# Rotary turn of queries and keys in the mixer: from products with a rotation matrix to small DMAs between partitions

## The chip, the cores and the metric

The kernel runs on one core of one Trainium2 chip. The metric is device time in microseconds (us) of one launch. Three timed runs of the kernel before gave 1842.23, 1841.44 and 1841.96, median 1841.96. In the text PE is TensorE, DVE is VectorE, ACT is ScalarE, POOL is GpSimd and SP is SyncE.

## The reference, cut to what matters

The program is a block of two transformer stacks on 512 tokens of width 1024, in float32: feed-forward, a mixer of dilated attention and pooling, feed-forward, then a retention layer and a stick-breaking attention layer. The change touches only the rotary embedding of the mixer's attention, 12 heads of 64 rows of which the first 16 turn:

```python
def apply_partial_rope(x, cos, sin):
    xf = x.astype(jnp.float32)
    half = ROT_DIM // 2                      # ROT_DIM = 16
    x1, x2 = xf[..., :half], xf[..., half:ROT_DIM]
    c, s = cos[None, :, None, :], sin[None, :, None, :]
    out = jnp.concatenate([x1 * c - x2 * s, x2 * c + x1 * s, xf[..., ROT_DIM:]], axis=-1)
    return out.astype(x.dtype)
...
    q = apply_partial_rope(q, cos, sin)
    k = apply_partial_rope(k, cos, sin)
```

The attention that follows uses q and k in scores, an exponential and a product with the values; its result is mixed over three groups of heads.

## The kernel before, in words

Features lie on the 128 partitions and the 512 tokens along the free dimension. A float32 product is made of three PE passes (`passes`, L2580 to L2582): each operand is split by ACT into a rounded high part and by DVE into the rest (`x_hi`, `x_lo`, `w_hi`, `w_lo`). Weights come in slabs of 128x2048: SP fetches a slab into a ring of two (`raw`), ACT writes `w_hi` (`prep`, L740), DVE writes `w_lo` (L1457), and PE uses it for two tiles of eight chunks of three passes.

The mixer does its attention in two halves, each with `qk(last)`, values, and `attend`. A half has six tiles of projected rows, named here (g, o): group g = 0, 1, 2 and o = 0 for queries, 1 for keys. A tile holds two heads, in partitions 0 to 63 and 64 to 127. In the half `qk(False)` the tiles (0,0) and (0,1) are projected together; in `qk(True)` the tile (0,0) was projected ahead, in a bank of `att`.

For each tile, in program order on each engine:

- PE projects the tile into a bank of PSUM (`acc`, four banks).
- ACT copies it, rounded, to `stage_hi` (`rope_split`, L761). DVE writes the rest to `stage_lo` (`rope_low`, L1481) and the tile times the cosines to `tmp` (`rope_cos`, L1796).
- PE, behind the projection of the next tile, multiplies both parts with the constant matrix `rot_r`, which exchanges rows 0 to 7 of a head with rows 8 to 15 and turns a sign (`rotate`, L2752 and L2753).
- DVE multiplies this product by the sines (L1805) and adds (L1808); ACT writes the rounded result (L972, L977, L980: `k_hi`, `q_pair`, `q_both` or `k_both`), and DVE the rest (L1811, L1814, L1819: `k_lo`, `q_pair`, `q_low` or `k_rest`). This is `rope_done`.

So `rope_done` of one tile stands behind `rope_split` and `rope_cos` of the next tile on ACT and DVE. An exception is the end of `qk(True)`: there `rope_done` of (2,0) comes ahead of the split of (2,1), and PE turns (2,0) in the middle of projecting (2,1), and (2,1) in the middle of the values. After the key tiles ((0,1) and (1,1)) ACT and DVE also prepare the next weight slab (`prep`).

POOL's queue then moves queries between partition halves (`q_head<-q_pair` and others), and PE's first scores of a half wait for these DMAs and for the last `k_lo`. Behind `rope_done` of (2,1) DVE prepares weights, forms operands, and takes the maxima of the first scores (`neg_max`, L1853), on which ACT's exponentials (L1013) and then PE wait. Every engine works its own list in order; the waits between engines are semaphores.

`rope_turned` and `rope_in`, which the change adds, lie over the same memory as `stage`. `stage` is used again by `attend` for the turned probabilities.

Of the kernel before, what the change touches and what calls it, by code (L numbers as in the profile page):

```python
# [24 lines left out]
P = 128  # L25
# [30 lines left out]
DIL = 4  # L56
UNITS = 2 * DIL
# [60 lines left out]
def block_kernel(nc, dram, out):  # L118
    with ExitStack() as ctx:
# [34 lines left out]
        rot_r = sb("rot_r", [P, P], F32R)  # L154
# [6 lines left out]
        signs = tmp[:, 4 * TOK:4 * TOK + 3 * P].rearrange("p (k c) -> p k c", k=3)  # L161
# [88 lines left out]
        with ExitStack() as scope:  # L250
# [13 lines left out]
            with ExitStack() as inner:  # L264
# [3 lines left out]
                va = sb("va", [P, TB, N_GROUPS * GROUP_HEADS, 2, HEAD], F32R, inner)  # L268
                stage = sb("stage", [P, 4 * KEYS], F32R, inner)
# [96 lines left out]
        stage_hi, stage_lo = stage[:, 0:2 * KEYS], stage[:, 2 * KEYS:]  # L366
# [73 lines left out]
        rest_clear = sem("rest_clear")  # L440
        h_back = sem("h_back")
# [196 lines left out]
        def _(pool):  # L638
# [26 lines left out]

            pool.wait_ge(park_landed, 16)
# [61 lines left out]
        def _(act):  # L728
# [230 lines left out]
            def rope_split(o, side=False):  # L959

                src = att[:, b.k % BANKS, :] if side else acc[:, u.k % BANKS, :]
                split_acc(stage_hi[:, o * TOK:(o + 1) * TOK], src, 1)
                s.next()
                (b if side else u).next()

            def rope_done(g, o):
                b.next()
# [15 lines left out]
            def qk(last):  # L983
                for g in range(N_GROUPS):
                    for o in range(2):
# [461 lines left out]
        def _(dve):  # L1447
# [332 lines left out]
            nc.vector.tensor_copy(rot_r[:], signs[:, 0, :])  # L1780
            nc.vector.tensor_copy(tri_r[:], signs[:, 1, :]).then_inc(att_free, BANKS)
            nc.vector.tensor_copy(ones_r[:], signs[:, 2, :]).then_inc(const_ready, 1)
# [11 lines left out]
            def rope_cos(o, side=False):  # L1794
                src = att[:, b.k % BANKS, :] if side else acc[:, u.k % BANKS, :]
# [4 lines left out]
            both, lows = Count(), Count()  # L1800
# [23 lines left out]
            def qk(last):  # L1824
                for g in range(N_GROUPS):
                    for o in range(2):
                        if (g, o) == (0, 0):
                            prep()
                            if not last:
                                rstd_of()  # L1830
                                dve.wait_ge(mix_landed, 6 * 16)
                                rope_low(0)

# [5 lines left out]
                        if last or (g, o) != (0, 0):  # L1839
                            rope_low(o, last and (g, o) == (0, 0))  # L1840
# [714 lines left out]
        def _(pe):  # L2555
# [192 lines left out]
            def rotate(o):  # L2748

                dst = side_bank()  # L2750
                cols = slice(o * TOK, (o + 1) * TOK)
                mm(dst, rot_r[:], stage_hi[:, cols], start=True, stop=False)  # L2752
                mm(dst, rot_r[:], stage_lo[:, cols], start=False, stop=True).then_inc(att_full, 1)  # L2753

            def qk(last, ahead=None):
                for g in range(N_GROUPS):
# [8 lines left out]
                    for o in range(2):  # L2765
                        if last and (g, o) == (N_GROUPS - 1, 1):
                            dst = bank()
                            for c in range(DC):
                                if c == DC // 2:
                                    pe.wait_ge(op_ready, op.at())  # L2770
                                    rotate(0)
                                    op.next(2)
# [97 lines left out]
            for i in range(4):  # L2870
# [3 lines left out]
                if i == 0:  # L2874
                    rotate_last()
# [535 lines left out]
```

## Time and profile before

| | us |
|---|---|
| median of three timed runs | 1841.96 |
| the profiled execution, its own time | 1841.76 |
| span of its trace | 1839.9 |
| PE busy in the span | 1823.6 (99%) |
| DVE busy | 1395.1 (76%) |
| ACT busy | 929.8 (51%) |
| POOL busy | 81.5 (4%) |

The profile is one execution. Start times count from the start of the span. Busy times leave out the issuing of DMAs. The mixer's two attention halves lie at about 358 to 460 us and 460 to 535 us. A row of the timeline gives start, duration, engine, line, operation, output <- input, shape and count; in brackets stands how long the engine was idle before it, and what released it.

### The profile page before, as it was taken

Reading aid. Unit: us, or ns where it says so; the run is one execution under the profiler, and the core shown is the slowest. Engines: PE = TensorE matmul, PEld = TensorE weight load, DVE = VectorE, ACT = ScalarE, POOL = GpSimd, SP = SyncE. Lnnn points to the kernel's source line nnn. Section 1 sums busy time; section 2 is a strip of 40 time slices with the busy share of each in tenths; the row PEclk is TensorE's granted clock in tenths of the full one; section 3 lists DMA queues with packets and bytes.
Section 4 is the critical chain, followed back from the end, with each engine's and each line's share of the span. In section 5 each row is a group of like instructions: output and inputs, shape, how many; then the busy total and the mean of one; then the engine's idle time right before and its main releaser. Section 6 shows DMA issues by size and latency. Waiting matters only on the chain.

```text
span 1839.9 us, 28202 instructions
## 1 busy us (share of the span) xinstructions
PE 1823.6 (99%) x11335; PEld 1632.7 (89%) x11341; DVE 1395.1 (76%) x1912; ACT 929.8 (51%) x1274; POOL 81.5 (4%) x109
## 2 busy tenths in 40 slices
PE   9999999999999999999999999999999999999997
PEld 7998998888889988988998899988888888888886
DVE  8875887888778878866888987776767776666566
ACT  6652664435355536643663555455547644444445
POOL 0000000020001000000000000000000000000000
PEclk9999999999999999999999999999999999999999
DMA  6744763462407535743753688732232222221223
GB/s 215 180 125 131 200 165 112 175 152 73 118 24 208 156 106 148 197 148 106 196 140 108 186 217 252 235 125 93 91 138 71 69 92 72 89 88 71 91 69 92
DMA packets 60594, 244.78 MB, mean 133 GB/s; under 512 B 6864, under 2 KB 9456, under 8 KB 49856
## 3 DMA queue, kind: packets, MB, share of 16 engines
q1 hardware_dynamic: 46016, 199.25, 32.3%
q0 software_dynamic: 14032, 43.38, 12.4%
q8 instruction: 80, 1.31, 0.3%
q10 hardware_dynamic: 432, 0.56, 0.1%
q14 instruction: 34, 0.28, 0.0%
HBM read 223.76 MB, written 13.11 MB: 129 GB/s over the span
## 4 chain that ended last, share of the span: by engine, by line
PE 93%; DVE 3%; ACT 1%; issue 1%; DMA 0%; DVEq 0%; ACTq 0%; POOL 0%
PE acc L2580 17%; PE acc L2582 17%; PE acc L2581 17%; PE acc L2588 9%; PE acc L2586 9%; PE acc L2587 9%; PE att L2581 2%; PE att L2582 2%; PE att L2580 2%; PE att L2588 1%; PE att L2586 1%; PE att L2587 1%; PE acc L2855 1%; PE acc L2830 1%; DVE w_lo L1457 0%
## 5 line engine op out<-in xcount | busy, mean ns | idle before, releaser
L1457 DVE TENSOR_TENSOR w_lo<-raw,w_hi 128x2048 fp32r<-128x2048 f32 (+1 forms) x106 | 238.9, 2254 | 56.8 <-ACT w_hi L740 56.5
L740 ACT ACTIVATE w_hi<-raw 128x2048 fp32r<-128x2048 f32 (+1 forms) x106 | 199.3, 1880 | 74.8 <-PE acc L2582 61.0
L2580 PE MATMUL acc<-x_hi,w_hi 128*128 128x512 f32 x488 | 193.1, 396 | 1.5 <-DVE x_lo L1520 1.2
L2582 PE MATMUL acc<-x_hi,w_lo 128*128 128x512 f32 x488 | 190.2, 390 | 0.0
L2581 PE MATMUL acc<-x_lo,w_hi 128*128 128x512 f32 x488 | 190.1, 390 | 0.0
L2586 PE MATMUL acc<-xt_hi,w_hi 128*128 128x256 f32 x684 | 189.1, 276 | 0.0
L2588 PE MATMUL acc<-xt_hi,w_lo 128*128 128x256 f32 x684 | 189.1, 276 | 0.0
L2587 PE MATMUL acc<-xt_lo,w_hi 128*128 128x256 f32 x684 | 189.0, 276 | 0.0
L839 ACT ACTIVATE tmp<-acc 128x256 f32<-128x256 f32 x228 | 86.9, 381 | 120.1 <-PE acc L2588 114.9
L2581 PE MATMUL acc<-g_lo,w_hi 128*128 128x512 f32 x352 | 137.0, 389 | 0.0
L2580 PE MATMUL acc<-g_hi,w_hi 128*128 128x512 f32 x352 | 137.0, 389 | 0.0
L2582 PE MATMUL acc<-g_hi,w_lo 128*128 128x512 f32 x352 | 136.9, 389 | 0.0
L2588 PEld LDWEIGHTS acc<-xt_hi,w_lo 128*128 128x128 f32 x684 | 128.4, 188 | 0.0
L2587 PEld LDWEIGHTS acc<-xt_lo,w_hi 128*128 128x128 f32 x684 | 128.4, 188 | 0.0
L2586 PEld LDWEIGHTS acc<-xt_hi,w_hi 128*128 128x128 f32 x684 | 128.3, 188 | 0.0
L2580 PEld LDWEIGHTS acc<-x_hi,w_hi 128*128 128x128 f32 x488 | 91.6, 188 | 23.1 <-issue 3.4
L2588 PE MATMUL acc<-x_hi,wc_lo 128*128 128x256 f32 x400 | 110.6, 276 | 0.0
L2586 PE MATMUL acc<-x_hi,wc_hi 128*128 128x256 f32 x400 | 110.6, 276 | 0.0
L2587 PE MATMUL acc<-x_lo,wc_hi 128*128 128x256 f32 x400 | 110.5, 276 | 0.0
L2581 PEld LDWEIGHTS acc<-x_lo,w_hi 128*128 128x128 f32 x488 | 91.6, 188 | 20.2 <-issue 1.4
L2582 PEld LDWEIGHTS acc<-x_hi,w_lo 128*128 128x128 f32 x488 | 91.6, 188 | 19.3
L796 ACT ACTIVATE wc_hi<-raw_c 128x1024 fp32r<-128x1024 f32 x57 | 60.4, 1059 | 50.9 <-PE acc L2588 50.9
(512 smaller groups left out, 5123.6 us busy)
## 6 DMA issues: line engine op xcount, KB each, us to landing
raw<-in_ffn_down SPq DMA_DIRECT2D x32, 704.0 KB, 4.1
raw_c<-in_ffn_seven SPq DMA_DIRECT2D x37, 512.0 KB, 5.3
raw<-in_ffn_seven SPq DMA_DIRECT2D x33, 512.0 KB, 4.4
raw<-in_ffn_seven POOLq DMA_DIRECT2D x33, 512.0 KB, 7.4
raw<-in_ffn_seven SPq DMA_DIRECT2D x37, 256.0 KB, 4.4
raw<-in_ret_values SPq DMA_DIRECT2D x8, 1024.0 KB, 4.8
raw<-in_ret_out SPq DMA_DIRECT2D x8, 1024.0 KB, 6.6
raw<-in_sb_v SPq DMA_DIRECT2D x8, 1024.0 KB, 4.8
```

The source lines that it names most:

```text
L740: nc.scalar.activation(w_hi[:, slot, at:at + cols], raw[:, slot, 0:cols], ACT.Copy).then_inc(w_hi_ready, 1)
L796: nc.scalar.activation(wc_hi[:, cols], raw_c[:, third, :], ACT.Copy).then_inc(wc_hi_ready, 1)
L839: nc.scalar.activation(dst, src, ACT.Copy).then_inc(snap_ready, 1)
L1457: tt(w_lo[:, slot, at:at + cols], raw[:, slot, 0:cols], w_hi[:, slot, at:at + cols].bitcast(F32), ALU.subtract).then_inc(w_ready, 1)
L2580: mm(dst, still[0], move[0], start=first, stop=False)
L2581: mm(dst, still[0], move[1], start=False, stop=False)
L2582: return mm(dst, still[1], move[0], start=False, stop=last)
L2586: mm(dst, still[0], move[0], start=first, stop=False, skip_group_check=True)
L2587: mm(dst, still[0], move[1], start=False, stop=False, skip_group_check=True)
L2588: return mm(dst, still[1], move[0], start=False, stop=last, skip_group_check=True)
L2830: last = nc.tensor.transpose(dst[i // TB][:, P * (i % TB):P * (i % TB) + P], tmp[:, at:at + P], ident[:])
L2855: last = mm(dst, va[:, k_blk, value_slot(g, head)].rearrange("p s d -> p (s d)"), turned_probs[:, k % 2, i].rearrange("p s q -> p (s q)"), ...
```

## The change

The rotated rows are no longer made by a product. ACT copies the tile unrounded to `rope_in`, waits for its own copy, and issues four DMAs of 8 partitions x 512 elements (16 KB) each on its own queue. They write the exchanged rows into `rope_turned`, whose other rows are zero. The sign has moved into the table of sines. DVE multiplies `rope_turned` by the sines, after a wait for the four DMAs of the tile. The 12 pairs of products, the 12 DVE subtractions for `stage_lo`, and the matrix `rot_r` with its cast are gone. POOL clears `rope_turned` (128x1024) once per half: behind the first feed-forward, and behind the last product of the first `attend`.

```diff
 # POOL
+            pool.wait_ge(seg_done, FFN_SEGS[0])
+            nc.gpsimd.memset(rope_turned[:], 0.0).then_inc(turned_clear, 1)
+            pool.wait_ge(turned_clear, 1)
             pool.wait_ge(park_landed, 16)
...
+            pool.wait_ge(mixed, UNITS)
+            nc.gpsimd.memset(rope_turned[:], 0.0).then_inc(turned_clear, 1)
             other_halves(1)
 # ACT
             def rope_split(o, side=False):
                 src = att[:, b.k % BANKS, :] if side else acc[:, u.k % BANKS, :]
-                split_acc(stage_hi[:, o * TOK:(o + 1) * TOK], src, 1)
+                act.wait_ge(seg_done, s.at(1))
+                nc.scalar.activation(rope_in[:, o, :], src, ACT.Copy).then_inc(rope_copied, 1)
...
+            def rope_turn(o, half):
+                act.wait_ge(rope_copied, copied.next())
+                act.wait_ge(turned_clear, half + 1)
+                for first in range(0, P, HEAD):
+                    for j in range(2):
+                        to, src = (slice(first + ROT * i, first + ROT * (i + 1)) for i in (j, 1 - j))
+                        act.dma_start(rope_turned[to, o, :], rope_in[src, o, :]).then_inc(turned_landed[o], 16)
...
                         rope_split(o, last and (g, o) == (0, 0))
+                        rope_turn(o, int(last))
                         if o == 1 and g < N_GROUPS - 1:
                             prep()
 # DVE
-            def rope_low(o, side=False):
-                cols = slice(o * TOK, (o + 1) * TOK)
-                src = att[:, b.k % BANKS, :] if side else acc[:, u.k % BANKS, :]
-                settle()
-                low(stage_lo[:, cols], src, stage_hi[:, cols])
             def rope_cos(o, side=False):
                 src = att[:, b.k % BANKS, :] if side else acc[:, u.k % BANKS, :]
+                settle()
+                dve.wait_ge(rope_copied, copied.next())
                 tt(t(o), src, rope_a[:, 0, :], ALU.mult).then_inc(att_free if side else acc_free, 1)
...
             def rope_done(g, o, split_after):
-                dve.wait_ge(att_full, b.next())
-                tt(t(2 + o), att[:, (b.k - 1) % BANKS, :], rope_a[:, 1, :], ALU.mult).then_inc(att_free, 1)
-                dve.wait_ge(att_free, b.at(BANKS))
+                dve.wait_ge(turned_landed[o], 4 * 16 * shifted[o].next())
+                link(tt(t(2 + o), rope_turned[:, o, :], rope_a[:, 1, :], ALU.mult))
 # PE
-            def rotate(o):
-                dst = side_bank()
-                cols = slice(o * TOK, (o + 1) * TOK)
-                mm(dst, rot_r[:], stage_hi[:, cols], start=True, stop=False)
-                mm(dst, rot_r[:], stage_lo[:, cols], start=False, stop=True).then_inc(att_full, 1)
...
-                        if (g, o) != (0, 0):
-                            pe.wait_ge(op_ready, op.at(0 if g else 1))
-                            rotate(1 - o)
```

On ACT, from the square root at the head of `qk(False)` (L768 before, L779 after) to the first weight slab behind the tile (1,1), the kernel before has:

```order
L768 ACTIVATE tmp<-att,eps 128x512
L761 ACTIVATE stage<-acc 128x512 x2
L740 ACTIVATE w_hi<-raw 128x2048
L980 ACTIVATE q_both<-tmp 64x512 x2
L761 ACTIVATE stage<-acc 128x512
L980 ACTIVATE k_both<-tmp 64x512 x2
L761 ACTIVATE stage<-acc 128x512
L740 ACTIVATE w_hi<-raw 128x2048
```

The same place on ACT in the changed kernel:

```order
L779 ACTIVATE tmp<-att,eps 128x512
L974 ACTIVATE rope_in<-acc 128x512
L987 DMA rope_turned<-rope_in 8x512 x4
L974 ACTIVATE rope_in<-acc 128x512
L987 DMA rope_turned<-rope_in 8x512 x4
L751 ACTIVATE w_hi<-raw 128x2048
L1002 ACTIVATE q_both<-tmp 64x512 x2
L974 ACTIVATE rope_in<-acc 128x512
L987 DMA rope_turned<-rope_in 8x512 x4
L1002 ACTIVATE k_both<-tmp 64x512 x2
L974 ACTIVATE rope_in<-acc 128x512
L987 DMA rope_turned<-rope_in 8x512 x4
```

Eight DMA issues now stand ahead of the first `w_hi`, and eight more ahead of the second, which follows the last row shown.

On DVE, at the end of `qk(True)` from the query tile (2,0) on, the kernel before has:

```order
L1805 TENSOR_TENSOR tmp<-att,rope_a 128x512
L1808 TENSOR_TENSOR tmp<-tmp 128x512
L1814 SCALAR_TENSOR_TENSOR q_pair<-tmp,q_pair 128x256 x2
L1481 TENSOR_TENSOR stage<-acc,stage 128x512
L1796 TENSOR_TENSOR tmp<-acc,rope_a 128x512
L1805 TENSOR_TENSOR tmp<-att,rope_a 128x512
L1808 TENSOR_TENSOR tmp<-tmp 128x512
L1811 SCALAR_TENSOR_TENSOR k_lo<-tmp,k_hi 128x512
L1457 TENSOR_TENSOR w_lo<-raw,w_hi 128x1536
```

And in the changed kernel:

```order
L1824 TENSOR_TENSOR tmp<-rope_turned,rope_a 128x512
L1826 TENSOR_TENSOR tmp<-tmp 128x512
L1832 SCALAR_TENSOR_TENSOR q_pair<-tmp,q_pair 128x256 x2
L1814 TENSOR_TENSOR tmp<-acc,rope_a 128x512
L1824 TENSOR_TENSOR tmp<-rope_turned,rope_a 128x512
L1826 TENSOR_TENSOR tmp<-tmp 128x512
L1829 SCALAR_TENSOR_TENSOR k_lo<-tmp,k_hi 128x512
L1480 TENSOR_TENSOR w_lo<-raw,w_hi 128x1536
```

One subtraction is gone, and the second product with the sines (the key tile (2,1)) reads `rope_turned`, whose rows come by DMAs issued only after ACT's copy of that tile.

## Rows read from the trace of the kernel before

**Rows 1.** The page, part 1 and part 4 (chain that ended last).

```profile
PE 1823.6 (99%) x11335; PEld 1632.7 (89%) x11341; DVE 1395.1 (76%) x1912; ACT 929.8 (51%) x1274; POOL 81.5 (4%) x109
PE 93%; DVE 3%; ACT 1%; issue 1%; DMA 0%; DVEq 0%; ACTq 0%; POOL 0%
```

**Rows 2.** Timeline of PE round the second rotation of `qk(False)`.

```profile
364.62 0.40 PE L2752 MATMUL att<-stage,rot_r 128*128 128x512 f32 x1
365.10 0.40 PE L2580 MATMUL acc<-x_hi,w_hi 128*128 128x512 f32 x1
```

**Rows 3.** The two longest entries of PE's waits, 345 to 535 us: total, times, longest.

```profile
PE att L2752 <- DVE stage L1481: 0.9, 2, 0.5
PE att L2814 <- DMA q_head<-q_pair: 0.8, 1, 0.8
```

**Rows 4.** Timeline of ACT and SP's queue: DMA issues on the hardware queues.

```profile
0.76 0.40 ACTq L925 DMA_DIRECT2D gains<-in_gains  x1
1.19 1.00 ACTq L927 DMA_DIRECT2D h<-in_x  x2
...
811.36 0.33 SPq L491 DMA_DIRECT2D tmp<-in_ffn_seven  x1
...
813.16 0.62 SPq L472 DMA_DIRECT2D raw<-in_ffn_down  x1
```

**Rows 5.** Issue to landing, of the lines L925 (36 KB) and L927 (256 KB).

```profile
DMA to landing us min/median/max: 1.7/1.7/1.7
DMA to landing us min/median/max: 4.1/4.7/5.2
```

**Rows 6.** Timeline of POOL, first half.

```profile
357.68 1.81 POOL L670 MEMSET q_head<- 64x2048 f32 x1
```

**Rows 7.** Timeline of ACT, first half.

```profile
358.31 1.91 ACT L740 ACTIVATE w_hi<-raw 128x2048 fp32r<-128x2048 f32 x1
...
370.74 1.27 ACT L980 ACTIVATE k_both<-tmp 64x512 fp32r<-64x512 f32 x2 [3.49 <-DVE tmp L1808]
...
425.72 0.84 ACT L1006 ACTIVATE va<-acc,r_tok 128x256 fp32r<-128x256 f32 x2 [0.24 <-PE acc L2582]
```

**Rows 8.** Timeline of DVE, first half.

```profile
361.71 2.28 DVE L1457 TENSOR_TENSOR w_lo<-raw,w_hi 128x2048 fp32r<-128x2048 f32 x1
...
373.48 0.69 DVE L1481 TENSOR_TENSOR stage<-acc,stage 128x512 fp32r<-128x512 f32 x1
...
374.69 2.28 DVE L1457 TENSOR_TENSOR w_lo<-raw,w_hi 128x2048 fp32r<-128x2048 f32 x1
...
389.01 2.29 DVE L1457 TENSOR_TENSOR w_lo<-raw,w_hi 128x2048 fp32r<-128x2048 f32 x1 [1.11 <-ACT w_hi L740]
...
424.17 0.68 DVE L1457 TENSOR_TENSOR w_lo<-raw,w_hi 128x512 fp32r<-128x512 f32 x1
```

**Rows 9.** Timeline of ACT, second half.

```profile
468.08 0.60 ACT L761 ACTIVATE stage<-acc 128x512 fp32r<-128x512 f32 x1 [3.85 <-PE acc L2582]
468.57 1.91 ACT L740 ACTIVATE w_hi<-raw 128x2048 fp32r<-128x2048 f32 x1
```

**Rows 10.** Timeline of DVE, second half.

```profile
483.50 2.28 DVE L1457 TENSOR_TENSOR w_lo<-raw,w_hi 128x2048 fp32r<-128x2048 f32 x1
...
496.94 0.69 DVE L1805 TENSOR_TENSOR tmp<-att,rope_a 128x512 f32<-128x512 f32 x1 [0.23 <-PE att L2753]
...
499.06 0.69 DVE L1811 SCALAR_TENSOR_TENSOR k_lo<-tmp,k_hi 128x512 fp32r<-128x512 f32 x1 [0.70 <-ACT k_hi L972]
```

**Rows 11.** Timeline of PE: first and third scores of the second half.

```profile
500.41 0.27 PE L2814 MATMUL att<-classes,ident_b 128*128 128x256 bf16 x1 [0.78 <-DMA q_head<-q_pair]
...
508.85 0.27 PE L2814 MATMUL att<-classes,ident_b 128*128 128x256 bf16 x1
```

**Rows 12.** Busy time by window: PE, PEld, DVE, ACT, POOL, then granted clock, DMA share, GB/s.

```profile
1831.00:1833.00 2.00, 0.00 (x0) 0.00 (x0) 1.44 (x4) 1.02 (x3) 0.59 (x1) 1.00 0.95 184
1835.00:1837.00 2.00, 0.00 (x0) 0.00 (x0) 0.00 (x0) 0.00 (x0) 0.00 (x0) 0.50 0.87 266
```

More of the change, by code:

```diff
@@ L56 @@
 DIL = 4
+ROT = HEAD // 8
 UNITS = 2 * DIL
@@ L153, in block_kernel @@
         mean_d = sb("mean_d", [P, P])
-        rot_r = sb("rot_r", [P, P], F32R)
         tri_r = sb("tri_r", [P, P], F32R)
@@ L268, in block_kernel @@
                 va = sb("va", [P, TB, N_GROUPS * GROUP_HEADS, 2, HEAD], F32R, inner)
+                with ExitStack() as under:
+                    rope_in = sb("rope_in", [P, 2, TOK], F32, under)
+                    rope_turned = sb("rope_turned", [P, 2, TOK], F32, under)
                 stage = sb("stage", [P, 4 * KEYS], F32R, inner)
@@ L440, in block_kernel @@
         rest_clear = sem("rest_clear")
+        rope_copied = sem("rope_copied")
+        turned_clear = sem("turned_clear")
+        turned_landed = [sem(f"turned_landed{o}") for o in range(2)]
         h_back = sem("h_back")
@@ L1779, in _ @@
             dve.wait_ge(const_landed, 4 * 16)
-            nc.vector.tensor_copy(rot_r[:], signs[:, 0, :])
-            nc.vector.tensor_copy(tri_r[:], signs[:, 1, :]).then_inc(att_free, BANKS)
-            nc.vector.tensor_copy(ones_r[:], signs[:, 2, :]).then_inc(const_ready, 1)
+            nc.vector.tensor_copy(tri_r[:], signs[:, 0, :]).then_inc(att_free, BANKS)
+            nc.vector.tensor_copy(ones_r[:], signs[:, 1, :]).then_inc(const_ready, 1)
             dve.wait_ge(const_ready, 1)
@@ L1838, in qk @@
                             rope_done(g, 0, 0)
-                        if last or (g, o) != (0, 0):
-                            rope_low(o, last and (g, o) == (0, 0))
                         rope_cos(o, last and (g, o) == (0, 0))
@@ L2765, in qk @@
                     for o in range(2):
[L2766 to L2772, printed above, removed]
-                                done = passes(dst, w(DC + c), (x_hi[:, c, :], x_lo[:, c, :]), c == 0, c == DC - 1)
-                            done.then_inc(seg_done, 1)
-                            continue
                         if g or last and o:
                             project(w, o * DC, x)
-                        if (g, o) != (0, 0):
-                            pe.wait_ge(op_ready, op.at(0 if g else 1))
-                            rotate(1 - o)
-                            op.next(2)
                         elif last:
                             gather(units_done, 1)
-            def rotate_last(behind=0):
-                pe.wait_ge(op_ready, op.at(behind))
-                rotate(1)
-                op.next(2)
+                op.next(2 * N_GROUPS)
             def gather(done, filled):
@@ L2908, in _ @@
             qk(True, ahead[0])
-            values(x, plain, {(0, DC - 1): lambda: rotate_last(1), (1, DC - 1): lambda: first_score(1),
+            values(x, plain, {(1, DC - 1): lambda: first_score(1),
                               (2, DC - 1): lambda: scores(1, 1)})
@@ L3357, in constants @@
     c["diag_neg"] = np.where(i >= j, f(NEG), f(0))
-    half = HEAD // 8
-    rot = np.zeros((P, P), f)
-    for m in range(P):
-        d = m % HEAD
-        if d < half:
-            rot[m + half, m] = -1
-        elif d < 2 * half:
-            rot[m - half, m] = 1
+    half = ROT
     c["fold"] = np.hstack([np.zeros((P, HEAD), f), np.vstack([np.eye(HEAD, dtype=f)] * 2), np.zeros((P, HEAD), f)])
-    c["signs"] = np.stack([rot, (i >= j).astype(f), np.ones((P, P), f)], 1)
+    c["signs"] = np.stack([(i >= j).astype(f), np.ones((P, P), f)], 1)
     pos = np.arange(TOK, dtype=f)
@@ L3373, in constants @@
             ang = pos * inv[m % HEAD % half]
-            cos[m], sin[m] = np.cos(ang), np.sin(ang)
+            cos[m], sin[m] = np.cos(ang), np.sin(ang) * f(1 if m % HEAD >= half else -1)
     c["rope_a"] = np.stack([cos, sin], 1).reshape(P, 2, P, DIL).transpose(0, 1, 3, 2).reshape(P, 2, TOK)
```

13 lines of the change are left out of this document (5 added, 8 removed).

## The prediction

> **What bounds the kernel now.** I read the page first: PE is busy for 99% of the span and carries 93% of the chain that ended last [rows 1]. So whatever leaves PE's list could be worth its full time, and whatever is added to DVE or ACT seems free. That is an average, so I then read PE's waits in the stage of the change: from 345 to 535 us the only waits of more than 0.2 us are 0.9 for the operands of the rotation and 0.8 for the queries' DMA [rows 3]. The reader should see two things: PE has almost no slack to lose, and each wait is short because DVE and ACT are just in time. The third view is the timelines of ACT and DVE. In the first half DVE works from 361.71 to 424.85 with hardly a gap that PE causes [rows 8]: its short gaps are round trips to ACT, as before the slab at 389.01. At 425.72 ACT is only 0.24 us ahead of PE [rows 7]. In the second half a run of ACT and DVE work goes from ACT's copy at 468.08, which PE released, to the last `k_lo` at 499.75 [rows 9, 10], and PE starts the first scores 0.7 us later [rows 11]. So the chain through ACT and DVE decides in both halves, and PE arrives together with it.
>
> **What goes.** Twelve rotations leave PE. One takes 365.10 - 364.62 = 0.48 us of its list [rows 2]; a matmul's own 0.40 overlaps with the next. That is 12 x 0.48 = 5.8 us, and 0.9 of waiting before two of them [rows 3]: 6.7 us for PE alone. DVE loses 12 subtractions of 0.69 [rows 8], start to start 0.6, about 0.7 of its list with the signal that each costs. The cast of `rot_r` is at 22 us and under other work: nothing.
>
> **What comes.** Each tile puts four DMA issues on ACT behind its copy. The trace has issues on ACT of 0.40 and 0.50 us, and four on SP in a row that take 813.16 - 811.36 = 1.80 us [rows 4]. All of these have 128 partitions; the new ones have 8. The durations hardly follow the size, so I take 1.8 us for four, plus 0.1 for ACT's wait for its own copy (my estimate: the hand-overs between engines in these rows are below 0.1). Ends: 0.33 each (SP's shortest), 1.35 for four; and 0.52 each (ACT's, rounded up), 2.1. If the cost is by partitions, 8 instead of 128, it would be near 0.1 each. An issue to landing took 1.7 us for 36 KB and 4.7 for 256 KB [rows 5]; for 16 KB I take 1.7, with 4.7 as the far end. The clearings of POOL stand behind work that ended, and the second must be over when ACT wants to issue at 461: POOL clears 64x2048 in 1.81 us [rows 6], so 1024 columns should take about 1 and surely below 2, from PE's last product of the half at 459; and ACT is idle for 3.85 us before 468.08 [rows 9], which covers the delay of its copies. Nothing for them.
>
> **First half.** All times are on the clock of the trace before. ACT: copy of (0,0) to 357.7, wait and issues to 359.6, copy of (0,1) to 360.2, issues to 362.1, `w_hi` 1.9 to 364.0. It was done at 360.2 [rows 7]. DVE starts `w_lo` at 364.05 instead of 361.71 [rows 8]: +2.3. On to the tile (1,1) one subtraction is gone: +1.6. There ACT, after `k_both`, now needs 0.6 copy + 0.1 + 1.8 + 1.9 = 4.4 us until `w_hi` is there. `k_both` ends at 372.0 before [rows 7] and 373.6 now, so `w_lo` starts at 378.05 instead of 374.69: +3.35. Two more subtractions go: the slab of 389.01 starts at 390.95, +1.95. Then the pooling is the same DVE and ACT chain as before, and its weights end at 426.8 instead of 424.85. The 0.24 us that ACT waited for PE [rows 7] absorb a part: **+1.7 us**. PE, 3.6 us ahead by then (six rotations and the missing wait), loses this lead in waits for weight slabs and goes on with the chain.
>
> **Second half.** ACT's copy at 468.08 is released by PE, so it starts level. Issues to 470.5, `w_hi` to 472.4 instead of 470.48: `w_lo` +2.0. Less one subtraction: +1.25. At (1,1) again 4.4 us after `k_both`: `w_lo` at 486.45 instead of 483.50 [rows 10], +2.95. Less one: the `k_lo` of (1,1) and the `q_pair` of (2,0) +2.1. ACT then copies (2,1) from 496.65 to 497.2 and issues until 499.1; the last DMA starts at 498.65 and lands 1.7 later, 500.35. DVE multiplies by the sines at 500.4 instead of 496.94 [rows 10], and the last `k_lo` ends at 503.2 instead of 499.75: **+3.45 us**. Queued behind that one DVE wait are the branch weights, three sums, the values and the two maxima, in all the chain that releases the third scores, at 508.85 before [rows 11]: also +3.45. PE meanwhile reaches the first scores at 496.2 (2.9 from six rotations and 0.5 of waiting less), waits 7 us, then has 8.2 us of work, done at 511.4; the third scores are released at 512.3. Its lead is gone here too.
>
> Sum: 1841.76 + 1.7 + 3.45 = 1846.9. The 7 us wait may cost more: with PE idle at the end of the trace, the granted clock is 1.00 and then 0.50 [rows 12], that is 2.4 and then 1.2 GHz. PE has 0.9 us in hand behind the wait; half speed over a third of its 8.2 us of work costs 2.7, which leaves 1.8 if the clock falls. I give that one chance in three, +0.6. Forecast: **1847.5**, 5.7 above the profiled execution and 5.5 above the median of the runs (the execution lies 0.2 below it).
>
> The Trainium skill (DMA: Bandwidth & Descriptors, section Issuing engines are not separate DMA queues) says that the time a sequencer needs to start a DMA is usually small relative to the DMA itself. Here it isn't: four issues take 1.80 against 1.7 to landing [rows 4, 5]. By the rule the issues would count little, as in the second rival.
>
> **Rivals.**
> 1. *All is hidden.* PE is at 99% and decides alone: 1841.76 - 6.7 = 1835.1. For it speaks the page [rows 1], and that `rope_done` comes a whole tile of projection after the copy. Against it: the tile (2,1) has no tile behind it, and 389.01 to 424.85 is DVE's own chain. 5%.
> 2. *Issues are cheap* (0.1 each, 0.4 for four), the case on the fast side of the chain. Then `w_hi` is never late, and DVE gains 0.4 at the first slab and 0.6 to 0.7 per tile: 2.1 at the end of the first half. In the second the missing subtractions are nearly used up by the landing of (2,1): DMAs from 494.1 land at 496.3, `k_lo` ends 0.5 earlier. 1841.76 - 2.6 = 1839.2. It decides where four issues take less than about 1.0 us. For it: 8 rows instead of 128. Against: 36 KB and 256 KB differ by a tenth of a microsecond on ACT [rows 4]. 20%.
> 3. *The clock falls.* PE's 8.2 us behind the wait take twice as long: it reaches the third scores at 503.25 + 16.3 = 519.5 instead of 512.3: 1846.9 + 7.2 = 1854.1. It needs the idle stretch to be long enough and the return slow; no row shows the return. 8%. The Trainium skill (TensorE: Matmul & The Clock Gate, its table of rules at the end) warns that a long idle gap between bursts of matmuls brings the clock down to half; by it the fall is certain here, and the forecast would be 1848.7 with the return as I took it.
> 4. *Landing is slow* (4.7 us beside the weight loads): the last sines wait 3.0 longer, in the first half the tile (2,0) about 2: 1846.9 + 5 = 1852. 12%.
>
> The forecast holds with 55%. Its own range comes from the ends of the issue cost. Three blocks of four issues stand in the deciding chain of each half, six in all: 5.15 - 6 x 0.45 = 2.5 at 1.35 us, 5.15 + 6 x 0.3 = 6.95 at 2.1 us, and up to 1.8 for the clock, so 1844.2 to 1850.5. The whole range to hold 8 in 10 takes in a part of the slow landing and of cheap issues: 1840.5 to 1853.5. A measurement of this kernel tells about 0.2%, 3.7 us, from no change. Faster by more (below 1838.3): rival 1 and a little of 2, 8%. Within: most of rival 2 and the low side of the forecast, 27%. Slower: 65%.
>
> **What would show it.** Timeline of ACT: four issues of 0.4 to 0.5 us behind each copy; at 0.1 rival 2 is right. DVE's slabs (before at 374.69 and 483.50) start 3 us late against ACT's copies. PE's waits in the stage grow from below 2 to some 13 us, the longest about 7 before the first scores of the second half, released by `k_lo`, with `turned_landed` behind it. If PE's waits stay below 3 us, the chain did not bind, and I am wrong. A granted clock below 1.00 in 500 to 515 us speaks for rival 3. Outside 345 to 535 us nothing should change.

## The result, and the profile after

| | before | after |
|---|---|---|
| median of 5 runs each, us | 1841.76 | 1862.49 |
| range of them, us | 1841.19 to 1842.23 | 1859.60 to 1863.01 |
| profiled execution, us | 1841.8 | 1859.6 |
| its span, us | 1839.9 | 1857.8 |

The ratio is 1.0105, 95% interval 1.0094 to 1.0117: the change makes the kernel 20.7 us slower. The direction was forecast, the size (5.7 us) was not, and the measured time lies outside the range given. The two profiled executions differ by 17.9 us in their spans, and that is the difference which the rows below can account for.

The page after, part 1 and part 4, against [rows 1]:

```profile
PE 1820.6 (98%) x11317; PEld 1629.8 (88%) x11317; DVE 1388.8 (75%) x1899; ACT 929.7 (50%) x1274; POOL 83.3 (4%) x111
PE 90%; DVE 4%; ACT 2%; issue 1%; ACTq 1%; DMA 1%; DVEq 0%
```

PE and DVE work less, as the change intends, and only POOL works more, 83.3 against 81.5 us. DVE, ACT, the issues and the DMAs have taken some 3% of the deciding chain from PE. PE's waits, 345 to 560 us (total, times, longest), against [rows 3]:

```profile
PE att L2802 <- DVE k_lo L1829: 13.9, 1, 13.9
PE acc L2594 <- DVE w_lo L1480: 9.3, 4, 3.7
```

The waits grew from 1.9 to 23.4 us. They have the two places that the prediction named, with 13.9 us in place of 7 before the first scores. (Each sum takes in 0.2 us for `o_even`, which is the same in both.) Next ACT's timeline, first half and (from 490.21) second half. Its rows of before are [rows 7, 9]; ACTq rows are its DMA issues, and 2.61 is the time of four of them.

```profile
357.79 3.23 ACTq L987 DMA_DIRECT2D rope_turned<-rope_in  x4
361.07 0.60 ACT L974 ACTIVATE rope_in<-acc 128x512 f32<-128x512 f32 x1 [3.31 <-issue]
361.70 2.61 ACTq L987 DMA_DIRECT2D rope_turned<-rope_in  x4
364.41 1.92 ACT L751 ACTIVATE w_hi<-raw 128x2048 fp32r<-128x2048 f32 x1 [2.74 <-PE acc L2596]
...
490.21 2.62 ACTq L987 DMA_DIRECT2D rope_turned<-rope_in  x4
492.93 1.92 ACT L751 ACTIVATE w_hi<-raw 128x2048 fp32r<-128x2048 f32 x1 [2.75 <-issue]
...
499.68 3.95 ACTq L987 DMA_DIRECT2D rope_turned<-rope_in  x4
503.68 0.63 ACT L994 ACTIVATE k_hi<-tmp 128x512 fp32r<-128x512 f32 x1 [4.03 <-issue]
...
508.47 2.67 ACTq L987 DMA_DIRECT2D rope_turned<-rope_in  x4
```

A block of four issues takes 2.6 to 3.95 us, not 1.8, and ACT does nothing beside it here. The block of tile (2,0), at 499.68, also holds `k_hi` of the tile before, which the prediction had not counted. DVE's timeline shows where this arrives, against [rows 8, 10]:

```profile
366.36 2.29 DVE L1480 TENSOR_TENSOR w_lo<-raw,w_hi 128x2048 fp32r<-128x2048 f32 x1 [3.90 <-ACT w_hi L751]
...
381.39 2.29 DVE L1480 TENSOR_TENSOR w_lo<-raw,w_hi 128x2048 fp32r<-128x2048 f32 x1 [3.15 <-ACT w_hi L751]
...
390.03 0.69 DVE L1829 SCALAR_TENSOR_TENSOR k_lo<-tmp,k_hi 128x512 fp32r<-128x512 f32 x1 [1.51 <-ACT k_hi L994]
...
391.84 0.69 DVE L1824 TENSOR_TENSOR tmp<-rope_turned,rope_a 128x512 f32<-128x512 f32 x1 [0.39 <-DMA rope_turned<-rope_in]
...
395.83 2.29 DVE L1480 TENSOR_TENSOR w_lo<-raw,w_hi 128x2048 fp32r<-128x2048 f32 x1 [1.12 <-ACT w_hi L751]
...
494.88 2.29 DVE L1480 TENSOR_TENSOR w_lo<-raw,w_hi 128x2048 fp32r<-128x2048 f32 x1 [3.16 <-ACT w_hi L751]
...
504.34 0.69 DVE L1829 SCALAR_TENSOR_TENSOR k_lo<-tmp,k_hi 128x512 fp32r<-128x512 f32 x1 [2.33 <-ACT k_hi L994]
...
505.88 0.69 DVE L1824 TENSOR_TENSOR tmp<-rope_turned,rope_a 128x512 f32<-128x512 f32 x1 [0.85 <-DMA rope_turned<-rope_in]
...
514.01 0.69 DVE L1824 TENSOR_TENSOR tmp<-rope_turned,rope_a 128x512 f32<-128x512 f32 x1 [4.54 <-DMA rope_turned<-rope_in]
...
516.12 0.69 DVE L1829 SCALAR_TENSOR_TENSOR k_lo<-tmp,k_hi 128x512 fp32r<-128x512 f32 x1 [0.70 <-ACT k_hi L994]
```

The slab of 389.01 [rows 8] starts at 395.83: +6.82 at the end of the first half's chain, of which 6.46 is still there when ACT makes the first copy that PE releases in the second (474.54 against 468.08 in [rows 9]). The last `k_lo` starts at 516.12 against 499.06 [rows 10]: +17.06.

The granted clock, by window (columns as in [rows 12]), and PE's first and third scores, whose first row of before is in [rows 11] by the other product of the pair:

```profile
384.00:386.00 2.00, 2.00 (x5) 1.56 (x6) 1.27 (x3) 0.95 (x2) 0.00 (x0) 0.50 0.63 152
...
502.00:504.00 2.00, 0.95 (x9) 0.75 (x7) 0.00 (x1) 0.33 (x1) 0.00 (x0) 1.00 1.01 208
504.00:506.00 2.00, 0.00 (x0) 0.00 (x0) 0.81 (x2) 0.30 (x1) 0.00 (x0) 1.00 0.18 32
506.00:508.00 2.00, 0.00 (x0) 0.00 (x0) 1.27 (x3) 0.67 (x2) 0.00 (x0) 0.63 0.00 0
...
510.00:512.00 2.00, 0.00 (x0) 0.00 (x0) 0.00 (x0) 0.00 (x0) 0.22 (x1) 0.50 0.89 182
...
516.00:520.00 4.00, 3.12 (x12) 2.66 (x13) 3.19 (x3) 2.19 (x4) 0.00 (x0) 0.50 0.00 0
520.00:522.00 2.00, 2.00 (x18) 2.00 (x17) 1.97 (x3) 0.00 (x0) 0.00 (x0) 0.95 0.82 250
```

```profile
516.88 0.61 PE L2802 MATMUL att<-band,ident_b 128*128 128x512 bf16 x1 [13.92 <-DVE k_lo L1829]
...
527.02 0.39 PE L2802 MATMUL att<-band,ident_b 128*128 128x512 bf16 x1
```

PE stops at 503, the clock goes to 0.50 (1.2 GHz) at 508 and is back near 1.00 at 520, 3 us after work resumed. First to third scores take 10.14 us, before 508.85 - 500.41 = 8.44 [rows 11]. The clock also fell in the first half, to 0.50 over 384 to 386, behind a wait of 3.7 us for `w_lo`; before, it was at 1.00 all through the stage. What that first fall cost, no run separates.

### The profile page after: what moved, and what is told of

It is laid out like the page before. It is cut to its first block, busy times and chain, and to the rows that moved or that the text cites. A ratio compares the mean times of both kernels' runs of the same rounds, so it can differ in the third digit from the quotient of the medians.

```text
span 1857.8 us, 28198 instructions
## 1 busy us (share of the span) xinstructions
PE 1820.6 (98%) x11317; PEld 1629.8 (88%) x11317; DVE 1388.8 (75%) x1899; ACT 929.7 (50%) x1274; POOL 83.3 (4%) x111
## 4 chain that ended last, share of the span: by engine, by line
PE 90%; DVE 4%; ACT 2%; issue 1%; ACTq 1%; DMA 1%; DVEq 0%
PE acc L2594 17%; PE acc L2595 16%; PE acc L2596 16%; PE acc L2601 9%; PE acc L2600 9%; PE acc L2602 9%; PE att L2595 2%; PE att L2596 2%; PE att L2594 2%; PE att L2601 1%; PE att L2602 1%; PE att L2600 1%; ACTq L987 1%; PE acc L2844 1%; PE acc L2819 1%
```

## The experiments

All are edits of the changed kernel unless said otherwise. The theory: the issues on ACT are the main cost, through what stands behind them; second the landing of a tile's rows where nothing covers it; third the clock. In the expectations, A is always the theory as it stood then.

**e1_no_dmas.** The four-issue loop of `rope_turn` is taken out, and with it DVE's wait; the exchanged rows stay zero.

```diff
-                for first in range(0, P, HEAD):
-                    for j in range(2):
-                        to, src = (slice(first + ROT * i, first + ROT * (i + 1)) for i in (j, 1 - j))
-                        act.dma_start(rope_turned[to, o, :], rope_in[src, o, :]).then_inc(turned_landed[o], 16)
...
-                dve.wait_ge(turned_landed[o], 4 * 16 * shifted[o].next())
```

> The changed kernel without its 48 small DMAs and without DVE's wait for them; the copies, the clearing by POOL and all else stay. Left out: the exchanged rows are zero, so the rotary turn is not computed. Theory A (the DMA issues hold ACT's queue and make the weight slabs and the last key tile late; the chain through ACT and DVE decides): the time falls to about 1839, 2.7 below the kernel before, since DVE's chain gains only its missing subtractions. Rival B (PE's list decides alone, the issues only disturb it): 1835.1, all 6.7 us of the removed products. If neither the issues nor the landing is the cause, the time stays near 1862.

Measured: 1840.61 (1839.80 to 1842.11), ratio 0.9992 [0.9982, 1.0001]. All the loss hangs on the DMAs. But even free of their cost the change gains almost nothing, though 6.7 us are gone from PE. I first read that as A, yet 2.8 us of what is missing was the clock, as e12_none_busy shows below.

**e2_two_dmas.** `for first in (0,):`, so two of four issues; the other head's rows are missing.

> The changed kernel with two of the four DMAs of a tile (the rows of the second head are not exchanged), the wait counted for two. A block of issues on ACT takes 1.3 us instead of 2.6. Theory A (issues on ACT's queue): seven to eight decisive blocks, each 1.3 shorter, less of the lost clock: about 1850. Rival C (the landing of the DMAs decides, 2 to 3.5 us from the last issue): one issue pair less matters only where DVE waits for a landing, twice, so 1859 to 1861.

Measured: 1850.90 (1848.86 to 1851.06), ratio 1.0046 [1.0029, 1.0063]. Half of the issues give back 11.6 of the 20.7 us: the cost goes with the number of issues.

**e3_16_rows.** Four issues of 16 partitions by half the columns, from and to the same partitions, in place of 8 by all (the rows are not exchanged).

> The changed kernel with four DMAs a tile as before and 16 KB each, but each moves 16 partitions x 256 elements on the same partitions instead of 8 x 512 to others (the rows are copied unexchanged). The question is why an issue takes 0.63 us instead of the 0.40 to 0.50 of the 128-partition DMAs. If a DMA over fewer than 16 partitions costs the queue more, the issue falls to 0.40 to 0.47, a block to 1.8, and the time to what I forecast for that cost, 1847 to 1850. If source and destination in SBUF or the queue of ACT in this stage make it slow, the issue stays at 0.63 and the time at 1862.

Measured: 1859.16 (1858.04 to 1861.52), ratio 1.0088 [1.0072, 1.0105]; 0.612 us for an issue (median) against 0.632. Twice the partitions change little. The interval overlaps that of the changed kernel.

**e4_sp_queue.** The four issues are made by SP between its loads of weights:

```diff
-                        act.dma_start(rope_turned[to, o, :], rope_in[src, o, :]).then_inc(turned_landed[o], 16)
+                        sp.dma_start(rope_turned[to, o, :], rope_in[src, o, :]).then_inc(turned_landed[o], 16)
```

> The changed kernel with the same 48 DMAs issued on SP's queue, in an order that keeps them between the weight loads as they fall due. Theory A: ACT's copies and weight slabs are on time again, so the first half gains about 2 on the kernel before; in the second the last key tile still waits for four issues (2.6) and a landing (2 to 3) behind its copy, about 3 later than before: 1840 to 1846. Rival C (landing and traffic of the small DMAs beside the weight loads): the moves are as late as before the edit, over 1855.

Measured: 1845.27 (1844.40 to 1846.01), ratio 1.0017 [1.0007, 1.0027]. An issue takes SP 0.625 us too, but nothing waits behind it: 17.2 us come back. DVE's timeline of this kernel, to compare with [rows 8, 10]:

```profile
386.81 2.29 DVE L1484 TENSOR_TENSOR w_lo<-raw,w_hi 128x2048 fp32r<-128x2048 f32 x1 [1.11 <-ACT w_hi L766]
...
490.78 0.69 DVE L1828 TENSOR_TENSOR tmp<-rope_turned,rope_a 128x512 f32<-128x512 f32 x1 [2.02 <-DMA rope_turned<-rope_in]
...
498.87 0.69 DVE L1828 TENSOR_TENSOR tmp<-rope_turned,rope_a 128x512 f32<-128x512 f32 x1 [4.50 <-DMA rope_turned<-rope_in]
...
500.99 0.69 DVE L1833 SCALAR_TENSOR_TENSOR k_lo<-tmp,k_hi 128x512 fp32r<-128x512 f32 x1 [0.69 <-ACT k_hi L999]
```

The first half's chain is now 2.2 us earlier than before (386.81 against 389.01). In the second the lead has grown to 3.85 us at the `k_lo` of (1,1) (488.06 against 491.91). Two waits for rows lose it again, 2.02 us at the tile (2,0) and 4.50 at the last tile, and the last `k_lo` is 1.93 us late.

**e8_weights_first.** Only the order on ACT: the split of the next weights ahead of the issues.

```diff
-                        rope_turn(o, int(last))
                         if o == 1 and g < N_GROUPS - 1:
                             prep()
+                        rope_turn(o, int(last))
```

> The changed kernel, with ACT's split of the next projection's weights (w_hi, 1.91 us) ahead of the key tile's four issues in place of behind them, so that DVE's w_lo no longer waits 3.90 us for it; the rows leave 1.9 us later. Theory A (the issues cost by what stands behind them on ACT): at the key tiles w_hi is 2.6 us earlier and the landing 1.9 us later, where DVE has work to cover it: some 2.5 us a tile come back at three of the tiles (1,1) and (2,1) and (0,1) of each half, less the last tile's later landing: 1850 to 1857. Rival B (the landing is what decides, the issue's place does not matter): 1862 to 1866, as slow as the change or slower.

Measured: 1851.39 (1849.82 to 1852.31), ratio 1.0047 [1.0031, 1.0062]. Moving one line gives back 11 us. ACT's timeline shows a reason that I had not expected:

```profile
361.89 1.91 ACT L751 ACTIVATE w_hi<-raw 128x2048 fp32r<-128x2048 f32 x1
362.03 2.61 ACTq L987 DMA_DIRECT2D rope_turned<-rope_in  x4
```

The issues run while the activation ahead of them works. I had expected the rows to leave 1.9 us later; they leave 0.14 us behind the start of `w_hi`. So a block costs ACT its full length only where an instruction behind it is due.

**e7_shapes.** The groups of four take six shapes in turn; `few` is 8 partitions, `table` the rotation table in DRAM. DVE gets other rows than the exchanged ones.

```diff
+                kind = turns[0] % 6
+                    if kind == 0:
+                        act.dma_start(room[few, o, :], rope_in[few, o, :]).then_inc(turned_landed[o], 16)
+                    elif kind == 1:
+                        act.dma_start(room[few, o, :], table[few, o, :]).then_inc(turned_landed[o], 16)
...
```

> The twelve tiles' groups of four issues on ACT take six shapes in turn: 8 partitions by 2 KB from SBUF, the same from DRAM, 16 partitions by 2 KB from SBUF, the same from DRAM, 128 partitions by 128 bytes from SBUF, the same from DRAM. The rows that DVE takes are then not the exchanged ones, so the values are others; the waits are the same. Theory A (an issue costs ACT more for a source in SBUF than for one in DRAM): some 0.61 to 0.63 us each from SBUF, 0.33 to 0.50 us from DRAM, whatever the rows. Rival B (it costs by the partitions, the 128-partition ones being the cheap ones): 0.63 us for 8 partitions of either source, under 0.5 us for 128 partitions of either source. Rival C (it costs by what stands ahead on the queue, the first of a group less than the later ones): the same in all six, with the later of a group dearer.

Measured: 1855.37 in a single run; what counts are its rows. The answers for the six lines, in ns min/median/max: 8 partitions, then 16, then 128, each from SBUF (`rope_in`) and from DRAM (`in_rope_a`):

```profile
L993 ACTq DMA_DIRECT2D rope_turned<-rope_in x8: 632/642/1264, 357.4 to 467.7; - x8
L995 ACTq DMA_DIRECT2D rope_turned<-in_rope_a x8: 287/312/324, 361.3 to 474.2; - x8
L997 ACTq DMA_DIRECT2D rope_turned<-rope_in x8: 555/612/1022, 370.3 to 484.4; - x8
L999 ACTq DMA_DIRECT2D rope_turned<-in_rope_a x8: 332/436/442, 375.1 to 488.3; - x8
L1001 ACTq DMA_DIRECT2D rope_turned<-rope_in x8: 522/626/1357, 383.7 to 498.1; - x8
L1003 ACTq DMA_DIRECT2D rope_turned<-in_rope_a x8: 352/452/453, 388.1 to 505.4; - x8
```

Theory A: 0.61 to 0.64 us from SBUF at any number of partitions, 0.31 to 0.45 from DRAM. No issue from DRAM (at most 0.453 us) reaches the shortest one from SBUF (0.522). In this run the query tiles have the source in SBUF and the key tiles that in DRAM, so by itself it can't tell source from tile. The changed kernel can: there both kinds of tile copy from SBUF, and both take 2.61 to 2.62 us for four where nothing lengthens them. So of what was varied it is the source in SBUF that makes an issue dear. Why the chip takes longer for it is not shown here.

**e10_small_heads.** GpSimd's last two copies of `q_head` carry 8 partitions instead of 64, so that they leave the DMA engines to the last tile's rows.

```diff
+                        rows = slice(own[j].start, own[j].start + 8) if a and g else own[j]
-                        pool.dma_start(q_head[j][own[j], :, g, :], q_pair[own[j], :, :]).then_inc(head_landed, 16)
+                        pool.dma_start(q_head[j][rows, :, g, :], q_pair[rows, :, :]).then_inc(head_landed, 16)
```

> The changed kernel, where in the second half GpSimd's last two copies of the query heads (q_head, 256 KB each, issued at 509.05 while the last tile's exchanged rows are under way) carry 8 partitions each in place of 64; the scores of those heads are computed from zeros for the rest. Theory A (the last tile's rows land 2.87 us behind the end of their issues because they share the DMA engines with those copies, share 0.81 to 0.97 over 510 to 513): the landing falls to 1.7 us or less, DVE's wait from 4.54 to about 3.4 us. Rival B (a row exchange takes 2.9 us by itself): the wait stays at 4.3 to 4.6 us.

One run of 1859.89 us, so the rows of its trace decide. The last block of issues and the DVE instruction that waits for it:

```profile
509.63 2.61 ACTq L988 DMA_DIRECT2D rope_turned<-rope_in  x4
```

```profile
513.64 0.69 DVE L1825 TENSOR_TENSOR tmp<-rope_turned,rope_a 128x512 f32<-128x512 f32 x1 [3.01 <-DMA rope_turned<-rope_in]
```

From the end of the issues to DVE it takes 513.64 - 512.24 = 1.40 us, in the changed kernel 514.01 - 511.14 = 2.87. The sharing costs 1.5 us there. The Trainium skill (DMA: Bandwidth & Descriptors, section Issuing engines are not separate DMA queues) says that DMAs of all engines run on the same 16 DMA engines and interleave. The trace agrees: GpSimd's copies and ACT's rows stood in each other's way, with a DMA share of 0.89 over 510 to 512, against 0.24 with the small copies.

**e11_two_queues.** e4_sp_queue with two of the last tile's four issues on ACT.

> e4_sp_queue (48 issues on SP's queue), with two of the four issues of the last tile (2,1) of each half on ACT, where nothing stands behind them but a step that waits for that tile itself. Theory A (an issue costs its 0.62 us one after another on a queue, and the last tile's issues are on the path): the block on each queue is 1.25 us in place of 2.5, DVE's wait of 4.50 us for the last tile falls by about 1.2 to 3.3 us, and the time is 1843.5 to 1844.5 against 1845.3. Rival B (the landing, not the issue, sets the last tile, so that rows issued earlier land no earlier): wait still 4.3 to 4.6 us, 1845 to 1846.

Measured: 1845.18 (1843.42 to 1846.99), ratio 1.0018 [1.0009, 1.0028]. Neither: DVE's wait fell from 4.50 to 3.86 us, half of what A said, and the time is the same as in e4_sp_queue. Part of what the issues save is taken by a later landing: from the end of the last issue to DVE it takes 498.40 - 495.02 = 3.38 us, in e4_sp_queue 498.87 - 496.05 = 2.82.

**e5_hybrid.** e4_sp_queue, but tiles (2,0) and (2,1) of the second half are rotated by PE, as before:

```diff
-                            rope_done(g, 0)
-                        rope_split(o, last and (g, o) == (0, 0))
+                            rope_done(g, 0, True)
+                        rope_split(o, last and (g, o) == (0, 0), last and g == N_GROUPS - 1)
...
+            def rotate(behind):
+                pe.wait_ge(op_ready, op.at(behind))
+                dst = side_bank()
+                mm(dst, rot_r[:], stage_hi, start=True, stop=False)
+                mm(dst, rot_r[:], stage_lo, start=False, stop=True).then_inc(att_full, 1)
```

> The 48 issues stand on SP's queue, as in e4_sp_queue, and in the second half alone tiles (2,0) and (2,1) are rotated by PE with a product as in the kernel before: their copy is again split for PE, their eight DMAs are gone and two of the twelve 0.48 us products are back. Theory A (what e4_sp_queue had left over was the landing of the last tile of the second half, 4.50 us of DVE idle before sines at 498.87, while its first half had gained 2.2 us and its second had lost it again): the second half's last tile takes as long as before, the first half's 2.2 us stay, PE's wait for k_lo falls from 8.9 to about 3 us, and the time is about 2 to 4 us under the kernel before, 1838 to 1840. Rival B (the 2.2 us of the first half are taken back in any case, by a later wait that does not hang on the rotation, such as a load or the end of DVE's row): no difference from before, 1841 to 1843.

Measured: 1839.19 (median of 11 runs, 1838.37 to 1842.00) against 1842.33 (15 runs, 1841.58 to 1843.16): ratio 0.9984 [0.9975, 0.9993]. It is faster than the kernel before, by 3.1 us. It leaves out nothing, but it is no longer the change as made: only ten of the twelve tiles go through DMAs, from SP's queue. PE's waits in the stage, and the last `k_lo`, 3.00 us earlier than in [rows 10]:

```profile
PE att L2786 <- DVE stage L1516: 2.1, 2, 1.6
PE acc L2615 <- DVE w_lo L1492: 1.9, 1, 1.9
PE att L2836 <- DMA q_head<-q_pair: 1.2, 1, 1.2
```

```profile
496.06 0.69 DVE L1850 SCALAR_TENSOR_TENSOR k_lo<-tmp,k_hi 128x512 fp32r<-128x512 f32 x1 [0.70 <-ACT k_hi L1007]
```

**e6_busy_wait and e9_busy_longer.** What the clock adds: products that nobody reads are put where PE waits, 48 in the one and 62 in the other.

```diff
+                if a:
+                    pe.wait_ge(att_free, b.at(2))
+                    for _ in range(48):
+                        mm(att[:, b.k % BANKS, :], ident_b[:], by_rows(band[:, 0:TB, :]), start=True, stop=True)
```

> The changed kernel, with 48 bf16 products of 512 columns put ahead of the second half's first scores, into a bank that the scores clear again, so that PE works (some 10 us) where it waited 13.9 us for k_lo. It leaves out nothing. Theory A (the wait costs by the late k_lo; the fallen clock adds only the 1.1 us by which the third scores moved more than k_lo did, 18.17 against 17.06): 1860.5 to 1862.5, 1 us less or nothing. Rival B (the halved clock is what makes the size of the loss, as the third rival had it, since PE also does its work behind the wait at half speed): 7 us less, 1855 to 1857.

Measured: 1862.27 (1861.14 to 1864.18), ratio 1.0111 [1.0095, 1.0126]. It says nothing on the clock: PE still waited 3.7 us behind them, and the clock fell all the same, as the next expectation says.

> As e6_busy_wait, with 62 products in place of 48: there they ended at 513.32 (10.53 us, 0.219 us each), PE waited 3.75 us more, and the granted clock still fell (0.59 over 516 to 520, 0.55 over 520 to 524), so that run did not hold the clock. Now they end near 516.4, PE waits about 0.6 us. It leaves out nothing. Theory A (the fallen clock adds only the 1.1 us by which the third scores moved more than k_lo): the granted clock stays at 1.00 over 504 to 524, and the time is 1860.5 to 1862. Rival B (the clock makes up several us of the loss, by what PE does at half speed behind the wait): 1855 to 1858.

Measured: 1860.23 (1858.06 to 1860.99), ratio 1.0097 [1.0080, 1.0114]. The clock was 1.00 in every window from 500 to 524. The first and third scores:

```profile
519.38 0.39 PE L2802 MATMUL att<-band,ident_b 128*128 128x512 bf16 x1 [0.77 <-DVE k_lo L1829]
...
528.03 0.39 PE L2802 MATMUL att<-band,ident_b 128*128 128x512 bf16 x1
```

From the one to the other it took 528.03 - 519.38 = 8.65 us in place of 10.14: in the profiled execution the clock adds 1.5 us to the loss, and rival B (5 us or more) falls. The price is not the same everywhere: in e10_small_heads, e3_16_rows and e6_busy_wait, whose clock fell too, the stretch took 10.82, 11.02 and 11.48 us. The interval of the times overlaps that of the changed kernel, so this rests on the rows. (The 18.17 us in these expectations sets one product of a pair against the other; 508.85 less the 0.23 between the two in a pair gives 18.40, so 1.3 us more than `k_lo`.)

**e12_none_busy and e13_sp_busy.** The same with 18 products in e1_no_dmas and 38 in e4_sp_queue. In e1_no_dmas PE had waited 4.3 us, and the granted clock was:

```profile
495.00:500.00 5.00, 2.60 (x10) 2.16 (x11) 4.17 (x4) 2.18 (x4) 0.00 (x0) 0.70 0.41 99
500.00:502.00 2.00, 2.00 (x11) 2.00 (x11) 2.00 (x3) 0.00 (x0) 0.00 (x0) 0.50 0.91 377
502.00:504.00 2.00, 2.00 (x12) 2.00 (x11) 1.42 (x3) 0.54 (x1) 0.00 (x0) 0.54 0.13 49
```

> e1_no_dmas (no exchange of rows at all, so those rows are zero) with 18 bf16 products of 512 columns (0.22 us each, 3.9 us in all, into a bank that the scores clear) ahead of the second half's first scores, where PE waited 4.3 us. In e1_no_dmas the first scores came at 497.40, 2.8 us earlier than before, but the third at 508.93, 0.3 later, with a granted clock of 0.70, 0.50 and 0.54 over 495 to 504. Theory C (there the halved clock behind a wait of only 4.3 us took back the whole gain, some 3 us, since PE, not DVE, sets the pace behind the wait): the clock stays at 1.00, the third scores come at about 506, and the time is 1837 to 1838, 3 us under e1_no_dmas (1840.6). Rival D (the gain is lost in another place, the clock costs at most 1 us): 1839.5 to 1841.

Measured: 1837.78 (1837.39 to 1838.53), ratio 0.9978 [0.9969, 0.9988], against 0.9992 [0.9982, 1.0001] for e1_no_dmas. Its windows and the third scores, which are two products of the same line further on (the record of the second is missing):

```profile
495.00:500.00 5.00, 4.56 (x32) 3.30 (x31) 4.28 (x4) 1.80 (x3) 0.00 (x0) 1.00 0.37 87
500.00:502.00 2.00, 1.93 (x16) 1.78 (x16) 2.00 (x4) 0.00 (x0) 0.00 (x0) 1.00 0.94 397
```

```profile
497.01 0.38 PE L2797 MATMUL att<-band,ident_b 128*128 128x512 bf16 x1 [0.44 <-DMA q_head<-q_pair]
505.44 0.39 PE L2797 MATMUL att<-band,ident_b 128*128 128x512 bf16 x1
```

First to third scores: 8.43 us, in e1_no_dmas 508.93 - 497.40 = 11.53. Theory C holds: useless work in a wait makes the kernel 2.8 us faster, because the clock stays up. The two intervals overlap a little, but the slowest run with the products (1838.53) is faster than the fastest without (1839.80).

> e4_sp_queue (issues on SP's queue) with 38 such products (8.3 us) where PE waited 8.9 us for the last k_lo. It leaves out nothing. From first to third scores it took 10.07 us there, at a granted clock of 0.50 to 504 and 0.85 to 508, against 8.57 in e5_hybrid and 8.65 in e9_busy_longer at 1.00. Theory C: the clock stays at 1.00 and 1.5 us come back: 1843.3 to 1844.2, against 1845.3. Rival D (DVE's chain behind k_lo sets the third scores, clock or not): 1845 to 1846.

Measured: 1843.90 (1843.13 to 1845.57), ratio 1.0010 [1.0001, 1.0020], clock 1.00, first to third scores 510.81 - 502.17 = 8.64 in place of 10.07 us. That is 1.4 us less than e4_sp_queue, as C says, though the intervals overlap. The Trainium skill (TensorE: Matmul & The Clock Gate, the table of rules at the end) warns against long idle gaps between bursts of matmuls. The traces agree: the clock was halved behind the waits of 13.9, 8.9 and 4.3 us, and stood at 1.00 from 490 to 512 in e5_hybrid, whose longest wait is 1.9. They show more: it fell also behind the 3.7 us in the first half of the changed kernel, and in e2_two_dmas, where PE worked again from 392.70 on behind a wait of only 2.0 us, it was 0.56 over 394 to 396.

## Why the prediction was wrong

The mechanism was the forecast one: PE's saved time is worth nothing in this kernel, the chain through ACT and DVE decides in both halves, and the loss stands in PE's waits. The step that failed is the price of the chain: the issue block was put at 1.8 us and took 2.6 to 3.95, six deciding blocks were counted where there are eight, and the last landing was put at 1.3 us and took 2.87. Up to the last `k_lo` the prediction gave +1.7 and +3.45, 5.15 us; measured are 17.06, so 11.9 are missing. They go as follows.

- **The issue block, 1.8 us for four.** The six blocks named as deciding took 3.23, 2.61, 2.61, 2.62, 2.62 and 2.67, 16.4 us in place of 10.8: **+5.6**. Also its far end of 2.1 was passed. All the rows read were loads from DRAM, and these copy from SBUF (e7_shapes: 0.62 against 0.31 to 0.45 us). The prediction weighed the number of partitions, which hardly matters, and did not weigh the kind of source. Its remark that the durations follow the size little did not help. A row that it showed, 0.62 us at 813.16 [rows 4], was no hint either: that is a load from DRAM, of which 32 take 0.33 us in the median, so one of the long single ones.
- **Six deciding blocks.** They are eight. With 3.13 and 3.95 us the block of (2,0) holds up `k_hi` of (1,1) (1.51 and 2.33 in place of 0.70 of idle time) and its rows come late (0.39 and 0.85): **+3.7**, found nowhere in the sum.
- **The last landing.** 2.87 us from the end of the issues to DVE in place of 1.3: **+1.6**. The prediction counted `q_head`'s copies neither as traffic beside it nor in time; e10_small_heads shows that they make the difference. The fourth rival (slow landing) had the mechanism with a larger price.
- **The missing subtractions.** For the five on the chain the sum took off 0.7, 1.4 (two), 0.75 and 0.85 us, 3.7 in all. They saved 0.58, 1.08, 0.60 and 0.58, 2.84 in all: **+0.9**. The first, for instance, is the stretch from the slab's `w_lo` to `k_both`, 370.74 - 361.71 = 9.03 us before [rows 7, 8] and 374.81 - 366.36 = 8.45 after.
- These make 11.8 of the 11.9.
- **The clock, +0.6.** It was one chance in three of 1.8 us. It fell, and cost 1.5 us (e9_busy_longer), so the price was near and the chance too low. The third rival (7.2) was far too dear, since the clock was back 3 us after PE resumed, not at the end of its 8.2 us of work, and DVE's chain covers a part.
- With the clock the rows make 18.4 us at the third scores, of which 17.9 are in the span. The median of the runs is another 2.9 us above the profiled execution (1859.6, the lowest of five). What differs between these executions is not shown, since one trace alone was kept. There is one sign: the profiled one had the highest mean granted clock of the five, 0.994 against 0.991 to 0.993, so a longer fall of the clock may be a part of it.

Right were: ACT's queue as the bottleneck (e4_sp_queue and e8_weights_first), the wait for `k_lo` with the rows behind it, and that the first half costs less than the second (6.5 against 10.6). One sum was off without effect: PE's lead at the end of the first half is 2.9 + 0.4 = 3.3 us, since of the 0.9 of waiting [rows 3] 0.5 lies in the second half, not 3.6. Cheap issues (the second rival) and the first rival fall with the measured 0.63 us. The sentence of the Trainium skill that the time to start a DMA is usually small relative to the DMA (DMA: Bandwidth & Descriptors, section Issuing engines are not separate DMA queues) again fails here: four issues take 2.61 us and the landing behind them 1.40 where nothing disturbs it.

One reading of mine was wrong for some time: e1_no_dmas at 1840.6 seemed to show that the time of PE's products is worth almost nothing even then. Without the fall of the clock it is 1837.8. Of the 6.7 us that PE saves, 4.2 could be had if the exchange were free (1841.95 - 1837.78, with the clock held up), and e5_hybrid gets 3.1 us.

## What to carry to other kernels

Price a DMA issue by what stands behind it on the issuing engine, and take the duration from a row with the same kind of source and target; put issues on a queue with nothing due behind them (here SP: 17 us), or behind a long instruction that covers them (11 us). Use a trip through a DMA only where a tile's work covers issue and landing, 4.0 to 5.6 us from the end of the copy to the use here, and leave the last tile of a stage to the engine at hand. When PE gets ahead, look at the granted clock before you call its saving worthless: the fall behind a wait of 4.3 us took back 2.8 us of gain.

## What the runs showed of the hardware that I had not expected

- An issue of a small DMA with its source in SBUF takes 0.61 to 0.64 us of the sequencer's time, on ACT for 8, 16 or 128 partitions and on SP for 8; from DRAM 0.31 us for 8 and 0.44 to 0.45 for 16 and 128.
- ACT's sequencer issues DMAs while an activation ahead of them still runs (361.89 and 362.03); the reverse is not so: what is behind the issues waits for all four.
- Blocks of issues are at times longer (3.1 to 3.95 us for four, single ones up to 1.7) with no cause that the trace names. The two long blocks of (2,0), at 386.19 and 499.68, lie where the DMA engines were busy for 0.90 to 1.01, with GpSimd's copies of `q_head` issued beside them (386.76, 500.35). But the block at 357.79 took 3.23 us at a share of 0.10 over 358 to 360, and no run tests it.
- Behind waits of 4.3 to 13.9 us PE worked at a granted clock of about 0.50 for 3 to 7 us (until 520 from 516.88, until 504 from 497.40), and behind a wait of 2.0 us in e2_two_dmas at 0.56 over 394 to 396; unread products in the wait kept it at 1.00 and, in e12_none_busy, made the whole kernel 2.8 us faster.
